# RWKV decoder step: the sample chunk's state products in 64x32 and 32x64 tiles, heads alternating

## The reference, cut to what matters

```python
def wkv7_scan(S0, r, w, k, v, kk, a):
    def step(S, inp):
        r_t, w_t, k_t, v_t, kk_t, a_t = inp
        sa = jnp.einsum('bhvk,bhk->bhv', S, -kk_t)
        S = (S * w_t[:, :, None, :] + sa[..., None] * (kk_t * a_t)[:, :, None, :]
             + v_t[..., None] * k_t[:, :, None, :])
        return S, jnp.einsum('bhvk,bhk->bhv', S, r_t)
```

## Time and profile before

| | us |
|---|---|
| median of 3 executions (2061.19 to 2070.82) | 2066.41 |
| the profiled execution | 2053.36 |
| its span, first to last instruction | 2051.6 |
| TensorE matmul busy / weight load busy | 1878.5 / 1719.3 |
| VectorE busy / ScalarE busy | 799.7 / 604.8 |
| mean granted TensorE clock | 0.949 of 2.4 GHz |

### The profile page before, as it was taken

How to read it: one execution, slowest core, us unless ns; L and a number is a source line. 1 busy time by engine, 2 the same in 40 slices (tenths; PEclk the granted TensorE clock), 3 DMA queues, 4 the chain that set the end, 5 groups by cost and what they waited for, 6 DMA issues and landing times.

```text
span 2051.6 us, 39597 instructions
## 1 busy us (share of the span) xinstructions
PE 1878.5 (92%) x18300; PEld 1719.3 (84%) x18300; DVE 799.7 (39%) x1116; ACT 604.8 (29%) x992; POOL 22.4 (1%) x37
## 2 busy tenths in 40 slices
PE   8999999878988899999999899767878999999996
PEld 6677789867967899999999799655537999999995
DVE  2545234523543444414442533534214443134422
ACT  4234034301334422122212422344534321222112
POOL 0000000001000000000000000100000000000000
PEclk9999999977979999999999999968998999999998
DMA  7211130002023334355432321151735222332121
GB/s 272 81 62 62 39 94 4 3 1 54 4 94 107 108 123 142 123 195 159 148 102 94 120 83 52 42 181 47 192 86 160 62 76 57 104 84 83 57 57 46
DMA packets 208821, 187.66 MB, mean 91 GB/s; under 512 B 13976, under 2 KB 199448, under 8 KB 207376
## 3 DMA queue, kind: packets, MB, share of 16 engines
q1 hardware_dynamic: 205440, 170.87, 27.1%
q0 software_dynamic: 3216, 14.26, 2.0%
HBM read 170.85 MB, written 41.13 MB: 103 GB/s over the span
## 4 chain that ended last, share of the span: by engine, by line
PE 61%; ACT 3%; DVE 3%; DMA 1%; issue 0%; POOL 0%; DVEq 0%; SPq 0%; POOLq 0%
PE banks L710 49%; PE banks L1227 3%; PE banks L683 2%; PE banks L997 2%; ACT arena L1479 1%; PE banks L1094 1%; PE banks L1185 1%; PE banks L1154 1%; PE banks L1112 1%; PE banks L1059 0%; DMA out<-arena 0%; POOL out L625 0%; DVE arena_r L2027 0%; DVE arena L2051 0%; ACT arena_r L1613 0%
## 5 line engine op out<-in xcount | busy, mean ns | idle before, releaser
L710 PE MATMUL banks<-arena_r 128*128 128x288 f32 x7440 | 1004.0, 297 | 12.9 <-DVE arena_r L2040 12.9
L710 PEld LDWEIGHTS banks<-arena_r 128*128 128x128 f32 x7440 | 997.6, 189 | 15.8 <-issue 13.1
L2027 DVE TENSOR_TENSOR arena_r<-ring,arena_r 128x2048 fp32r<-128x2048 f32 (+2 forms) x84 | 166.8, 1987 | 278.5 <-ACT arena_r L1613 278.5
L669 PE MATMUL banks<-arena,ring 128*128 128x288 f32 (+2 forms) x808 | 199.8, 409 | 0.9 <-ACT mkt L1349 0.7
L1613 ACT ACTIVATE arena_r<-ring 128x2048 fp32r<-128x2048 f32 (+2 forms) x84 | 140.0, 1668 | 199.4 <-PE banks L710 199.3
L669 PEld LDWEIGHTS banks<-arena,ring 128*128 128x128 f32 (+2 forms) x808 | 150.6, 187 | 48.6 <-issue 1.0
L997 PE MATMUL banks<-consts,arena 128*128 128x128 f32 (+3 forms) x548 | 88.9, 310 | 60.1 <-DMA arena<-in_cache_mem 18.8
L997 PEld LDWEIGHTS banks<-consts,arena 128*128 128x128 f32 (+3 forms) x548 | 67.4, 160 | 84.9 <-issue 30.0
L837 PE MATMUL banks<-arena 64*64 64x64 f32 x3312 | 114.6, 220 | 7.2 <-DVE arena L1833 3.0
L1303 ACT ACTIVATE arena<-banks 128x576 f32<-128x576 f32 (+1 forms) x77 | 49.8, 648 | 230.5 <-PE banks L669 112.2
L837 PEld LDWEIGHTS banks<-arena 64*64 64x64 f32 x3312 | 107.2, 136 | 11.0 <-DVE arena L1833 3.8
(11 more groups left out here) (212 smaller groups left out, 1406.9 us busy)
## 6 DMA issues: line engine op xcount, KB each, us to landing
ring<-in_w_ffn_in SPq DMA_DIRECT2D x88, 512.0 KB, 5.1
ring<-in_w_ffn_out SPq DMA_DIRECT2D x32, 704.0 KB, 4.5
out<-in_cache_win_g SPq DMA_DIRECT2D x16, 1016.0 KB, 7.6
ring<-in_a_w_in SPq DMA_DIRECT2D x10, 1024.0 KB, 5.0
arena<-in_cache_win_g SPq DMA_DIRECT2D x80, 128.0 KB, 5.9
arena<-in_cache_mem SPq DMA_DIRECT2D x16, 512.0 KB, 4.6
arena<-in_cache_win_g SPq DMA_DIRECT2D x16, 512.0 KB, 6.0
out<-in_cache_win_g SPq DMA_DIRECT2D x8, 1008.0 KB, 7.3
```

Of the source, the lines that this page charges most:

```text
L669: last = mm(banks[0:m, s + a, 0:HALF], w[0:parts, k, c0:c0 + m], x[0:parts, k, a * HALF:(a + 1) * HALF], start=(k == 0), stop=(k == nk - 1))
L710: last = mm(banks[:, s + a, 0:HALF], w[i][:, k, c0:c0 + P], x[j][:, k, a * HALF:(a + 1) * HALF], start=(k == 0 and m == 0), stop=(k == nk ...
L2027: last = v.tensor_tensor(lo, ring[:, n % RING, 0:nk * w], hi.bitcast(F32), ALU.subtract)
```

## The change

- `from_states` replaces the 8-long groups of the sample chunk: a product has 32 columns of weights (4 sequences x 8 tokens; the array tile is 64 rows x 32 columns), and the order goes over the sequence within its half, then the half `g`, then the head `i`. The tile of the next product is so always another one, and four of them take turns. The terms with Lak, Lrb, Lrk follow as 64x64 tiles with heads alternating.
- The masks have 4 x 32 columns twice (256 per `c`) in place of 512.
- dS: K x V and B x SA accumulate in one PSUM place. Each product takes 32 tokens (32 rows) and 256 moving columns, 48 products in place of 24. VectorE makes both masked copies before TensorE begins, scales `s0t` while TensorE works, and adds each increment once (6 additions of 512 columns in place of 12).
- So that the increments come out already scaled, the token factors A and K of the sample columns are multiplied by the decay before they are turned (12 VectorE products of 64 columns, new semaphore `tokens_scaled`).
- `turn_states` and the groups of the prompt chunks (`head_pair`) alternate the heads; dS of a prompt chunk takes its K term first.

```diff
-        masked = at(A_CL + CM * NB * HD, CM, NB, HD)
+        masked_t = at(A_CL + CM * NB * HD, CM, NB, 32)
+        masked_v = [at(A_CL + CM * NB * HD + q * CM * 4 * HD, CM, 4, HD) for q in range(2)]
...
-                    for i in range(2):
-                        for b in range(NB):
+                    for b in range(NB):
+                        for i in range(2):
                             last = turned_head(bank + c % 2, b * HD, src(b, c, i), i)
...
             def prepare(n, j):
-                for x in (A, K, V):
-                    turn(lambda c, q: x[hp(q), c, cols(j)])
+                if j == SAMPLE:
+                    pe.wait_ge(tokens_scaled, 1)
+                    for x in (o_buf[0], on_buf[0]):
+                        turn(lambda c, q: x[hp(q), c, :])
+                    turn(lambda c, q: V[hp(q), c, cols(j)])
+                else:
+                    for x in (A, K, V):
+                        turn(lambda c, q: x[hp(q), c, cols(j)])
...
-            def group(out, terms):
-                for m, (a, b) in enumerate(terms):
-                    last = mm(out, a, b, start=(m == 0), stop=(m == len(terms) - 1))
+            def head_pair(bank, c, terms):
+
+                for m, (lhs, rhs) in enumerate(terms):
+                    for i in range(2):
+                        last = mm(banks[hp(i), bank, c * C:(c + 1) * C], lhs(i), rhs(i), start=(m == 0), stop=(m == len(terms) - 1))
+                return last
+
+            def from_states(bank, c, rest):
+
+                for b4 in range(4):
+                    for g in range(2):
+                        for i in range(2):
+                            b = 4 * g + b4
+                            r0 = HD * i + 32 * g
+                            mm(banks[r0:r0 + 32, bank, c * C:(c + 1) * C], masked_t[hp(i), c, b, :], s0t[hp(i), c, b, :],
+                               start=(b4 == 0), stop=False)
+                for m, (lhs, rhs) in enumerate(rest):
+                    for i in range(2):
+                        last = mm(banks[hp(i), bank, c * C:(c + 1) * C], lhs(i), rhs(i), start=False, stop=(m == len(rest) - 1))
                 return last
...
+                def products(bank, chan, rest):
+                    for c in range(CM):
+                        terms = [(lambda i, x=x, c=c: x[hp(i), c, :], lambda i, y=y, c=c: y[hp(i), c, :]) for x, y in rest]
+                        if sample:
+                            last = from_states(bank, c, terms)
+                        else:
+                            last = head_pair(bank, c, [(lambda i: chan[hp(i), c, cols(j)], lambda i: state[hp(i), n % 2, c, :])] + terms)
+                    return last
                 def outputs_of_chunk():
...
+                    products(7, R, [(Lrb, sa_buf), (Lrk, V_)]).then_inc(o_psum, 1)
...
+                last = products(6, KK, [(Lak, V_)])
                 last.then_inc(u_psum, 1)
...
                     outputs_of_chunk()
-                    for q, tok in enumerate((B_, K_)):
-                        pe.wait_ge(masked_ready, 3 + q)
-                        for c in range(CM):
-                            m = q * CM + c
-                            if m >= 2:
-                                pe.wait_ge(dsm_free, m - 1)
-                            for i in range(2):
-                                last = mm(banks[hp(i), 4 + m % 2, :], tok[hp(i), c, :],
-                                          masked[hp(i), c, :, :].rearrange("p b v -> p (b v)"), start=True, stop=True)
-                            last.then_inc(dsm_psum, 1)
-                    pe.wait_ge(s0_scaled, 1)
+                    pe.wait_ge(masked_ready, 4)
+                    for c in range(CM):
+                        if c >= 2:
+                            pe.wait_ge(dsm_free, c - 1)
+                        for g in range(2):
+                            for q, tok in enumerate((K_, B_)):
+                                for i in range(2):
+                                    t0 = HD * i + 32 * g
+                                    last = mm(banks[hp(i), 2 * (c % 2) + g, 0:256], tok[t0:t0 + 32, c, :],
+                                              masked_v[q][t0:t0 + 32, c, :, :].rearrange("p b v -> p (b v)"), start=(q == 0), stop=(q == 1))
+                        last.then_inc(dsm_psum, 1)
+                    pe.wait_ge(dsm_free, CM)
                     turn_states(4, lambda b, c, i: s0t[hp(i), c, b, :], st_t, st_out)
...
+            for buf, x in ((o_buf[0], A), (on_buf[0], K)):
+                for c in range(CM):
+                    ins = v.tensor_tensor(buf[:, c, :].rearrange("p (b t) -> p b t", b=NB), x[:, c, TP:T].rearrange("p (b t) -> p b t", b=NB),
+                                          each(decay_end[:, c, 8:16], TS), ALU.mult)
+            ins.then_inc(tokens_scaled, 1)
...
                     dve.wait_ge(o_psum, 1)
                     dve.wait_ge(sa_sb, 1)
-                    mask_rows(sa_buf)
-                    for m in range(2 * CM):
-                        if m == CM:
-                            dve.wait_ge(dsm_psum, CM)
-                            mask_rows(prep[0][2])
-                        dve.wait_ge(dsm_psum, m + 1)
-                        s = s0t[:, m % CM].rearrange("p b v -> p (b v)")
-                        ins = v.tensor_tensor(s, banks[:, 4 + m % 2, :], s, ALU.add)
-                        ins.then_inc(dsm_free, 1)
-                    dve.wait_ge(dsm_free, 2 * CM)
+                    mask_rows(masked_v[0], prep[0][2])
+                    mask_rows(masked_v[1], sa_buf)
                     for c in range(CM):
                         ins = v.tensor_tensor(s0t[:, c], s0t[:, c], each(decay_end[:, c, 8:16], HD), ALU.mult)
                     ins.then_inc(s0_scaled, 1)
+                    dve.wait_ge(s0_scaled, 1)
+                    for c in range(CM):
+                        dve.wait_ge(dsm_psum, c + 1)
+                        s = s0t[:, c].rearrange("p (g b) v -> p g (b v)", g=2)
+                        v.tensor_tensor(s, banks[:, 2 * (c % 2):2 * (c % 2) + 2, 0:256], s, ALU.add).then_inc(dsm_free, 1)
```

More of the change, by code:

```diff
@@ L431, in trunk @@
         s0_in, s0_t, s0_ready = sem("s0_in"), sem("s0_t"), sem("s0_ready")
-        masked_ready = sem("masked_ready")
+        masked_ready, tokens_scaled = sem("masked_ready"), sem("tokens_scaled")
         turned, turned_out = sem("turned"), sem("turned_out")
@@ L919, in _ @@
                     pe.wait_ge(s_new, n)
[L921 to L924, removed]
-                def outputs_of_chunk():
-                    for c in range(CM):
-                        for i in range(2):
[L929 to L932, removed]
+                def products(bank, chan, rest):
[6 more added lines that the diff above has]
+                    return last
+                def outputs_of_chunk():
+                    products(7, R, [(Lrb, sa_buf), (Lrk, V_)]).then_inc(o_psum, 1)
                 if sample:
                     pe.wait_ge(masked_ready, 1)
[L936 to L939, removed]
+                last = products(6, KK, [(Lak, V_)])
                 last.then_inc(u_psum, 1)
@@ L969, in _ @@
                     for c in range(CM):
-                        for i in range(2):
-                            last = group(banks[hp(i), 6, c * C:(c + 1) * C],
-                                         [(B_[hp(i), c, :], sa_buf[hp(i), c, :]), (K_[hp(i), c, :], V_[hp(i), c, :])])
+                        last = head_pair(6, c, [(lambda i: K_[hp(i), c, :], lambda i: V_[hp(i), c, :]),
+                                                (lambda i: B_[hp(i), c, :], lambda i: sa_buf[hp(i), c, :])])
                     last.then_inc(ds_psum, 1)
@@ L1858, in _, with mask_batches, mask_rows @@
             dve.wait_ge(s0_t, CM)
-            def mask_batches(src, out=masked):
-                inb = const("in_batch").rearrange("p (b t) -> p b t", b=NB)
+            def mask_batches(src):
+                inb = const("in_batch").rearrange("p (g b t) -> p g b t", g=2, b=4)
                 for c in range(CM):
-                    ins = v.tensor_tensor(masked[:, c], src[:, c, TP:T].unsqueeze(1).broadcast_to([P, NB, C]), inb, ALU.mult)
+                    halves_ = src[:, c, TP:T].rearrange("p (g t) -> p g t", g=2).unsqueeze(2).broadcast_to([P, 2, 4, 32])
+                    ins = v.tensor_tensor(masked_t[:, c].rearrange("p (g b) t -> p g b t", g=2), halves_, inb, ALU.mult)
                 ins.then_inc(masked_ready, 1)
-            def mask_rows(src):
+            def mask_rows(dst, src):
                 for c in range(CM):
-                    ins = v.tensor_tensor(masked[:, c], over(src[:, c, :], NB), each(const("of_batch"), HD), ALU.mult)
+                    ins = v.tensor_tensor(dst[:, c], over(src[:, c, :], 4), each(const("of_batch"), HD), ALU.mult)
                 ins.then_inc(masked_ready, 1)
@@ L2183, in constants @@
     put("ids", s == q)
```

(4 more changed lines are left out.)

4 lines of the change are left out of this document (1 added, 3 removed).

## The result

The changed kernel takes 1998.14 us (median of 4 executions, 1986.35 to 2006.08), the kernel before 2063.80 (4 executions, 2052.84 to 2070.82): ratio 0.970, 95% interval 0.9662 to 0.9737. The prediction said 2020 with a range of 2006 to 2040; the direction was right, the time lies 8 us under the range. The profiled execution of the changed kernel took 2002.46 us with a span of 2000.7, against 2053.36 and 2051.6: 50.9 us less.

A forecast was written before the change was run, and what follows sets the result against it. Bound: a serial handover between TensorE, VectorE and ScalarE in the sample stage, with one-tile products and a fallen clock. Gain 48.0+1.0-2.5 = 46.5 us off the 2066.4 median gives 2020 us, range 2006 to 2040.

The forecast's parts named there:

- U: First group of sample products: four tiles at once, starting at the low clock, 7.0 us in place of 10.81.
- masks, O: VectorE's smaller masks, then the sample output products on four tiles, clock mostly up: 2.3 and 6.5 us.
- masks for dS: VectorE makes all 12 masks for the sample state increments at once before TensorE starts them: 4.3 us.
- dS to the turning back: Sample state increments, up to four products at once, with VectorE's scaling and additions: 428.0 to 438.0 us.
- A change of shape: Switching between 64x32 and 64x64 tiles on TensorE costs 0.09 us; 23 changes are 2 us.
- Rival 1: The clock stays at 1.2 GHz through the sample stage: gain 33 us, 2033 us; chance 0.18.
- rival 2: Issue or shared rows hold the sample stage to two tiles at once: gain 42 us, 2025; chance 0.13 alone.
- rival 3: Slower: the prompt chunks come to run at 1.2 GHz, 8.8 us more each, 2090 if all eight; chance 0.02.
- rival 4: Nothing changes: TensorE's window for starting products of other tiles is too short; 2066 us, chance 0.02.
- The step to the median: Whole kernel: gain subtracted from the 2066.4 us median, not the profiled execution 13 us under it, giving 2020.
- The 2.5 us for issue: Allowance in U and O for TensorE perhaps not issuing records at 15 ns: 2.5 us off the gain.
- The 1.0 us in the prompt chunks: Gain from alternating heads in groups of three terms, about 0.1 us in each of 8 chunks: 1 us (0 to 3).

The follow-up runs named there:

- e1: The changed kernel run again with no edit: 2000.55 us against 2053.14 for the kernel before, ratio 0.9752.
- e10: The changed kernel run a third time with no edit, beside e9: 2005.41 us against 2054.26 for the kernel before, ratio 0.9754.
- e5: The changed kernel with the 64x64 terms first in every second column tile, so fewer changes of tile shape: 1987.63 us, one execution.
- e4: The changed kernel with the half g varying faster than K or B in the increments: 1998.03 us, one execution.
- e3: The changed kernel with state products issued head by head and half by half, four in a row on one tile: 2019.57 us, one execution.
- e9: The changed kernel with the edits of e5, e6, e7, e8 and the order of e4 together: 1994.52 us against 2054.26 for the kernel before, ratio 0.9694.
- e8: The changed kernel with the six stores of sample states spread over the prompt chunks instead of issued at once: 2000.94 us, one execution.
- e6: The changed kernel with the six VectorE scalings of G moved behind the masks: 2008.07 us, one execution.
- e2: The kernel before with only the heads alternating in the sample groups and the turning of states, 64x64 tiles kept: 2023.43 us, ratio 0.9857.
- e7: The changed kernel with 60 unread products added in TensorE's wait for masks before the increments: 1997.76 us, one execution.

## Why the mechanism was right and the time wrong

The steps, profiled execution against profiled execution:

| step | predicted us | measured us |
|---|---|---|
| start of U | 407.9 | 408.50 (turning began 1.6 later than before) |
| U | 7.0 | 6.6 (408.50 to the mask at 415.10) |
| masks, O | 2.3, 6.5 | 2.25, 5.83 |
| masks for dS | 4.3 | 4.17 |
| dS to the turning back | 10.0 | 10.95 |
| turning back and its copies | 6.6 | 6.51 |
| `prepare` | 5.1 | 5.12 |
| first prompt chunk | 449.8 | 449.97 |

All of it stands within 1 us. U did start at 1.2 GHz in this profile and came back within it, O did keep the clock, dS did not. That the last line agrees to 0.2 us is luck: the stage began 1.6 us later than before and was 1.4 shorter than forecast (55.1 in place of 56.5 us; 53.7 and 53.2 in e1 and e10). A change of shape cost 0.13 us by the difference of 0.85 to ten rounds of 58 ns, 0.10 by e5, for 0.09 predicted. Rival 1 (low clock throughout) did not come (its 8.1 and 9.4 us at 1.2 GHz need 0.14 us a change of shape, which no row showed; in e4 a column tile of U at the low clock took 1.42 us, 8.5 for six), rival 2 fell with 14 ns a record, rival 3 with a clock of 0.98 in the prompt chunks, rival 4 with e3 against the changed kernel.

What failed, of the 21.8 us between 2019.9 and 1998.1:

1. *The step to the median*, 13.0 us. "The profiled execution is 13 us under the median of those shown, which I lay to where the clock falls elsewhere; off the median, 2066.4-46.5 = 2020". In 22 further executions of the kernel before, beside e1 and e9, the medians are 2053.1 and 2054.3, the profiled execution's own 2053.4. The first three were high, by chance or by their chip; the figure from the profiled execution, 2006.9, was the better one.
2. *The size of the gain*, 4.4 us: 50.9 between the profiled executions, 46.5 forecast. *The 2.5 us for issue* were not there (14 ns a record); without them the sum says 49.0. They had been worked out from U and O at 2.4 GHz (4.6 and 5.3 us) but were put on top of 7.0 and 6.5, which allowed for the low clock already. O took 5.83. *The 1.0 us in the prompt chunks* was not there either: from the first chunk to the copy of the last state 94.6 us, 94.2 before, with the new pause in it; without the pause, in e8, 91.6.
3. *The scatter of the changed kernel*, 4.3 us: its median lies that far under its profiled execution, which the forecast left out.
4. *The range.* Its low end joined the largest gain to the fastest of three executions of before, 2061. Executions of one kernel spread over 10 to 26 us in these comparisons, so a lower execution had to be allowed for. From the profiled execution the same gain gives 1998.

The rest of the 65.7 us in the first result is not in the sample stage. Two things behind it vary between executions of the same code. One: in a feed-forward stage the records of 288 columns stand 133 or 130 ns apart for the whole stage. Changed kernel, line 711, 200 us in each feed-forward stage; count, PEclk, DMA share, GB/s:

```profile
760.00:960.00 200.00, 200.00 (x1502) 1.00 0.49 162
1650.00:1850.00 200.00, 200.00 (x1541) 1.00 0.30 84
```

and e5, 1987.63 us, the fastest profiled execution:

```profile
760.00:960.00 200.00, 200.00 (x1541) 1.00 0.49 160
1650.00:1850.00 200.00, 200.00 (x1541) 1.00 0.31 86
```

200 us over 1502 is 133 ns, over 1541 130: 9.5 us in a stage of 440. Of the 24 stages in the twelve profiled executions 5 were quick ones (changed kernel second, e4 second, e5 both, e10 first), at the same granted clock. The kernel before has one profile here, with none. Two: from the copy of the last state to the first product of the next feed-forward stage (line 711) it took 53.3 us in the changed kernel's profile, 52.1 in e6, 51.8 in e9, 46.0 to 48.5 in the other nine, the code being the same. The clock falls at other places: its mean there is 0.67 to 0.73 in the three long ones, 0.83 in e1, e2, e8 and e10.

So the profiles' 50.9 us are 49.4 of the sample stage (104.5 to 55.1) less the 1.6 by which it began later, minus 0.4 in the prompt chunks, minus 5.3 in the attention behind them, plus 9.5 in the second feed-forward stage, and 0.7 less in between. Only the sample stage and the pause in the chunks are shown to be the change's; that the sum lies near the 48.9 and 52.6 us of the other comparisons is chance in part. What chooses 130 or 133 ns, and whether the change makes the quick one more frequent, is open: the changed kernel's own profiles had none quick in e1 and one of two in the others, too few to say. The three intervals of the ratio have 0.9723 to 0.9737 in common, a gain of 54 to 57 us, while the two larger comparisons alone centre on 51.

## What to carry to other kernels

Count tiles of the array, not products. In these traces a record of 64 columns holds its tile for 58 ns at 2.4 GHz (a float32 product is two records). Two or four tiles ran at once where consecutive products wanted different tiles; with four products in a row for the same tile (e3) most of it was lost. Order the loops so that the tile varies fastest, and put terms of one shape side by side (0.1 us a change).

Look at the wait ahead of a stretch as well as at the stretch. In every profile of the changed kernel the increments stood behind a wait of 4.2 us and ran at a mean clock of 0.61 to 0.84; where the wait was taken away (e7, e9) they ran at 1.00. But the clock was worth something only until VectorE became the limit, at 9.0 us.

Where executions scatter by 10 us or more, lay a gain that was worked out from a profile on that profile's own time, let the range be as wide as the scatter, and take several profiles of the unedited kernel before laying a difference of 1 or 2 us to an edit.

## What the runs showed of the hardware that was not expected

- Four tiles of 64x32 take records of 64 columns at 14 ns each, with a weight load for each, for 32 records on end (0.65 us). The Trainium skill, "TensorE: Matmul & The Clock Gate", under "Wait — 56ns, not 53.3ns?", has about 25 ns as the least distance from start to start; the trace differs, and the measurement decides.
- Runs of four products on one 64x32 tile, 36 us long in e3, did not bring the clock back from 1.2 GHz; with four tiles in turn it came back within 4 us in the changed kernel (408.5 to 412.4) and within 7 in e4.
- A burst of stores by GpSimd (1.6 MB, DMA engines 98% busy) stopped TensorE for 1.0 to 2.2 us in nine profiles, with no semaphore between them. TensorE's packet of instructions came 6.9 to 8.1 us after the one before in place of 3.3 to 4.7, and TensorE went on 1.2 to 1.6 us after it had landed.
- Records of 288 columns stood 133 or 130 ns apart for a whole feed-forward stage at the same granted clock of 1.00, differently from execution to execution: 9.5 us a stage.
